# The MLA score matmuls of a page group cut in two, the first half and the values ahead of the eighth page's keys

## The chip, the cores and the metric

The kernel runs on one core of a Trainium2 chip. The metric is the device time of one execution in microseconds (us). The program is written by hand, engine by engine: each engine runs its own instruction stream, and the streams meet only at semaphores. Every engine works through its stream in order, so a wait holds back all that stands behind it on that engine.

## The reference, cut to what matters

The reference is one step of a two-layer decoder over a prompt of 1024 positions and a sample of 8 sequences with 8 new positions each. The change touches one part: the attention of the 8 sequences over their cached pages (32 pages of 128 positions each, in each layer).

```python
def page_step(carry, inp):
    phys, j = inp
    c_blk = cache_ckv[layer, phys]                  # 128 x 256
    kpe_blk = cache_kpe[layer, phys]                # 128 x 32
    k = _mla_keys(c_blk, kpe_blk, pos, w_uk, g_k)   # RMS norm over [c_blk @ w_uk, kpe], then rotation
    sc = jnp.einsum('bthd,bphd->bhtp', q, k).astype(jnp.float32) * MLA_SCALE
    return _online_update(carry, sc, c_blk), None   # running maximum, running sum, p @ c_blk
```

The kernel never forms the normed keys. It folds the query into the latent space (`qt`), takes the scores from the page itself, and multiplies them afterwards by one factor for each position and head. That factor needs the sum of squares of `c_blk @ w_uk`, so the product is still made for every page, for its squares alone.

## The kernel before, in words

Each layer has a prompt stage, then the sample stage, then the output projection. The sample stage goes through 32 groups (`k` = 0 to 31) of G = 8 pages (`j` = 0 to 7), four groups to a sequence; both layers together have 64 groups. In a group, with "page 1" for `j` = 0 and so on:

- **TensorE** (`pe_group`, L1837 to L1869) turns pages two at a time (`turn_pair`, L1784, 4 transposes), and makes the keys of each page (`keys`, L1797: 2 matmuls of 512 columns, which the profile shows as 4 records). The next pair is turned two pages ahead of its use; the next group's first pair is turned ahead of page 8's keys (L1854). The rotated positional keys are transposed at page 2 (L1860), the last group's maxima at page 4 (`maxima_T`, L1831), the maxima are spread over the partitions at page 6 (`maxima_over`, L1835). Behind page 8's keys stand all scores of the group (`scores_of`, L1813 and L1815: for each page 6 matmuls of 64 columns with 64 weight columns, 12 records of the profile) and then the values of the last group (`values`, L1826: 8 matmuls with 64 weight columns, 16 records). Weights of all keys and turns are 128 columns wide, those of scores and values are 64 wide. `sample_step` (L1668) puts other small pieces of the sample's work between the pages.
- **ScalarE** copies each turned pair out of PSUM (L785), squares the keys (L806), and in the next group takes the exponentials of the scores at page 6 (`softmax`, L817 and L818), behind page 6's squaring and ahead of page 7's. L818 ends with the semaphore `pp_ready`, on which `values` waits. At the group's end it makes a logarithm and an exponential for the root (L810, L811).
- **VectorE** reduces the squares (L1299). After page 8's it computes the factor (L1304 to L1310), waits for `ps_ps`, the end of the scores, multiplies the scores out of PSUM bank 4 (L1316) and takes the maxima (L1318, `pm_ready`). Then it adds the last group's values to the accumulator (`gather`, L1342), and begins the next group with the sum of squares of the positional keys (L1297). `softmax` at pages 4 and 6 has the running maximum (L1327 to L1332) and the subtraction (L1335).
- **SyncE** loads pages into a ring of 4 groups. A group's slot is reloaded when `ring_free` tells that its values are done.

`keys` of page j waits for the squaring of page j - 2 (two PSUM banks), and the squaring of page j waits for VectorE's reduction of page j - 2 (two SBUF buffers). `scores_of` waits for `rotT_evac`, which ScalarE gives at page 3, and in group 0 for `qt_ready`, which VectorE gives at page 7 after copying the folded query (L1211, waiting for L1696 of TensorE at page 6). In group 3 ScalarE has four pieces of gate work, the last of them (L760) behind L818, and VectorE has two (L1241, L1244).

After group 31, TensorE turns the first rows of the mixed output (`turn_rows(0)`, L1422), then `maxima_T(31)` and the output projection (L1890). The projection waits for VectorE's copy of the turned rows (L1351), which stands on VectorE behind all of group 31 and the `gather` of group 30.

The few lines that fix TensorE's order at a group's end:

```python
                        if j == G - 1 and k + 1 < DB * NG:
                            turn_pair(k + 1, 0)
                        keys(k, j)
...
                    scores_of(k)
                    if k:
                        values(k - 1)
```

Of the kernel before, what the change touches and what calls it, by code (L numbers as in the profile page):

```python
# [29 lines left out]
DB, DT = 8, 8  # L30
# [31 lines left out]
G = 8  # L62
NG = PAGES // G
# [29 lines left out]
def build(nc, a, out):  # L93
    ctx = ExitStack()
    with ctx:
# [3 lines left out]
        s = type("Semaphores", (), {n: ctx.enter_context(nc.semaphore(n)) for n in SEMAPHORES})  # L99
# [107 lines left out]
        def pcT(q):  # L207

            q %= 5
            return pairs_r[:, q, :] if q < 3 else pairs_x[:, q - 3, :]  # L210
# [34 lines left out]
        def pages_of(k):  # L245

            return cring[:, k % NG, :, :] if k < DB * NG - 2 else late[:, k - (DB * NG - 2), :, :]
# [1151 lines left out]
        def _(pe):  # L1399
            mm, tp = pe.matmul, pe.transpose  # L1400

            def halves(out, lhsT, rhs, T, start, stop):

                for c in range(0, T, 64):
                    ins = mm(out[c:c + 64], lhsT[:, c:c + 64], rhs, start=start, stop=stop)
                return ins
# [57 lines left out]
            for L in range(DEPTH):  # L1464
# [38 lines left out]
                for t in range(NT):  # L1503
# [22 lines left out]
                    for c in range(2):  # L1526
                        ins = tp(ps[:, 6, 256 + c * P:256 + c * P + T], mq[0:T, c * P:c * P + P], ident[0:T, 0:T])
                    ins.then_inc(s.mqT_ps, 1)
                    if pm_:
# [5 lines left out]
                        for h in range(MH):  # L1535
                            w = slice(MD * (h % 2), MD * (h % 2) + MD)
                            ins = mm(ps[:, 6 + h % 2, NM * (h // 2):NM * (h // 2) + NM], mqT[w, h // 2, :], mkT[w, h // 2, :], start=True, stop=True)
# [11 lines left out]
                    for c in range(2):  # L1549
                        ins = tp(ps[:, 2, c * P:c * P + T], ck[0:T, c * P:c * P + P], ident[0:T, 0:T])  # L1550
# [21 lines left out]
                    for c in range(2):  # L1572
                        ins = mm(ps[0:T, 0, :], cT[:, c, 0:T], w_uk[:, c, :], start=c == 0, stop=c == 1)
                    ins.then_inc(s.kn_ps, 1)
                    if pm_:
                        pe.wait_ge(s.mp_ready, m + 1)
                        for j in range(8):
                            ins = tp(ps[:, 6 + j // 4, (j % 4) * P:(j % 4) * P + P], pt[:, 0, j * P:j * P + P], ident[:])
                        ins.then_inc(s.mpT_ps, 1)
                    pe.wait_ge(s.cq_ready, n + 1)  # L1580
                    for c in range(3):
                        ins = tp(ps[:, 3, c * P:c * P + T], cq[0:T, c * P:c * P + P], ident[0:T, 0:T])
# [7 lines left out]
                    for e in range(2):  # L1590
                        for c in range(3):
                            ins = mm(ps[0:T, 2 + e, 0:4 * QK], cqT[:, c, 0:T], w_uq[:, c, 4 * QK * e:4 * QK * e + 4 * QK], start=c == 0, stop=c == 2)
                    ins.then_inc(s.q_ps, 1)

                    if pm_:
# [3 lines left out]
                        for h in range(MH):  # L1599
                            for c in range(2):  # L1600
                                ins = halves(ps[:, 5, 256 + MD * h:256 + MD * h + MD], ptT[:, 2 * h + c, :], mv[:, c, MD * h:MD * h + MD], P, c == 0, c == 1)
                        ins.then_inc(s.mo_ps, 1)
                        pe.wait_ge(s.k_ready, n + 1)
                        for h in range(H):
                            ins = tp(ps[0:QK, h // 4, (h % 4) * P:(h % 4) * P + P], qk[:, 1, QK * h:QK * h + QK], ident[:])
# [3 lines left out]
                        for h in range(H):  # L1609
                            ins = tp(ps[0:QK, 2 + h // 4, (h % 4) * P:(h % 4) * P + P], qk[:, 0, QK * h:QK * h + QK], ident[:])  # L1610
                        ins.then_inc(s.kqv_ps, 1)
                        pe.wait_ge(s.kT_evac, m + 1)
                        for c in range(2):
                            ins = mm(ps[:, 1, :], cT[:, c, :], w_uv[:, c, :], start=c == 0, stop=c == 1)
# [19 lines left out]
                        for h in range(H):  # L1634
                            nh = m * H + h
                            pe.wait_ge(s.p_ready, nh + 1)
                            for j in range(t + 1):
                                ins = tp(ps[:, j // 4, (j % 4) * P:(j % 4) * P + P], pt[:, h % 2, j * P:j * P + P], ident[:])  # L1638
# [19 lines left out]
                            for j in range(t + 1):  # L1658
                                ins = halves(ps[:, 2, VD * h:VD * h + VD], ptT[:, j, :], vv[:, j, VD * h:VD * h + VD], P, j == 0, j == t)
# [113 lines left out]
                def turn_pair(k, q):  # L1773

                    n = (L * DB * NG + k) * (G // 2) + q
                    g = k % NG
                    if q == 0:
                        pe.wait_ge(bulk_in[g], 32 + ((L * DB * NG + k) // NG + 1) * 2 * G * 16)
                    if n >= 2:

                        pe.wait_ge(s.pcT_evac, n - 1)
                    for j in range(2):
                        for c in range(2):
                            ins = tp(ps[:, q % 2, j * R + c * P:j * R + c * P + P], pages_of(k)[:, 2 * q + j, c * P:c * P + P], ident[:])  # L1784
                    ins.then_inc(s.pcT_ps, 1)

                def keys(k, j):

                    np_ = (L * DB * NG + k) * G + j
                    pe.wait_ge(s.pcT_evac, np_ // 2 + 1)  # L1790
                    if np_ >= 2:

                        pe.wait_ge(s.pkn_sq, np_ - 1)
                    page = pcT(k * (G // 2) + j // 2)
                    for c in range(2):
                        o_ = (j % 2) * R + c * P
                        ins = mm(ps[:, 2 + j % 2, :], page[:, o_:o_ + P], w_uk[:, c, :], start=c == 0, stop=c == 1)  # L1797
                    ins.then_inc(s.pkn_ps, 1)

                def scores_of(k):  # L1800

                    n0, b = L * DB * NG + k, k // NG
                    pe.wait_ge(s.rotT_evac, n0 + 1)
                    if k == 0:
                        pe.wait_ge(s.qt_ready, L + 1)
                    for j in range(G):
                        page = pcT(k * (G // 2) + j // 2)
                        for c in range(3):
                            for half in range(0, P, 64):
                                so = ps[half:half + 64, 4, 64 * j:64 * j + 64]  # L1810
                                if c < 2:
                                    o_ = (j % 2) * R + c * P + half
                                    ins = mm(so, page[:, o_:o_ + 64], qt[:, c, 64 * b:64 * b + 64], start=c == 0, stop=False)  # L1813
                                else:
                                    ins = mm(so, rotT[:, j // 4, half:half + 64], qrz[:, j % 4, 64 * b:64 * b + 64], start=False, stop=True)  # L1815
                    ins.then_inc(s.ps_ps, 1)

                def values(k):

                    n0, g = L * DB * NG + k, k % NG  # L1820
                    pe.wait_ge(s.pp_ready, n0 + 1)
                    if n0:
                        pe.wait_ge(s.pacc_ready, n0)
                    for i in range(G):
                        e = 64 * (i % 2)
                        ins = mm(ps[e:e + 64, 6, 0:RW], psb[:, k % 2, 64 * i:64 * i + 64], pages_of(k)[:, i, :], start=i < 2, stop=i >= G - 2)  # L1826
                    ins.then_inc(s.ring_free, 1)

                def maxima_T(k):
                    pe.wait_ge(s.pm_ready, L * DB * NG + k + 1)  # L1830
                    tp(ps[:, 7, 256:384], pm, ident[:]).then_inc(s.pmT_ps, 1)  # L1831
# [5 lines left out]
                def pe_group(k):  # L1837

                    n0 = L * DB * NG + k
                    if k == 0:  # L1840
                        pe.wait_ge(s.q_ready, NT * L + TP + 1)
                        turn_pair(0, 0)
                    for j in range(G):
                        sample_step(k, j)
                        if j % 2 == 0 and j + 2 < G:
                            if j:
                                keys(k, j)
                                turn_pair(k, j // 2 + 1)
                            else:
                                turn_pair(k, 1)  # L1850
                                keys(k, j)
                            continue
                        if j == G - 1 and k + 1 < DB * NG:
                            turn_pair(k + 1, 0)  # L1854
                        keys(k, j)
                        if j == 1:

                            pe.wait_ge(s.kpe_rot, n0 + 1)
                            for c in range(2):
                                ins = tp(ps[:, 7, c * P:c * P + P], krot[:, k % 2, c * P:c * P + P], ident[:])  # L1860
                            ins.then_inc(s.rotT_ps, 1)
                        if j == 3 and k:
                            pe.wait_ge(s.rotT_evac, n0 + 1)
                            maxima_T(k - 1)
                        if j == 5 and k:
                            maxima_over(k - 1)
                    scores_of(k)
                    if k:
                        values(k - 1)  # L1869

                for k in range(DB * NG):
                    pe_group(k)
# [42 lines left out]
                for b in range(DB):  # L1915
                    for c in range(2):
                        o_ = (2 * b + c) * 64
                        ins = mm(ps[:, 6 + o_ // 512, o_ % 512:o_ % 512 + 64], acc[:, b, c * P:c * P + P], fold[:, 0:64], start=True, stop=True)  # L1918
# [4 lines left out]
                for h in range(H):  # L1923
                    for c in range(2):
                        ins = mm(ps[0:TS, 5, VD * h:VD * h + VD], latT[:, (c * H + h) * TS:(c * H + h) * TS + TS], w_uv[:, c, VD * h:VD * h + VD], start=c == 0, stop=c == 1)
# [10 lines left out]
                for k in range(KD):  # L1936
                    for c in range(2):
                        ins = mm(ps[TS * c:TS * c + TS, 2, :], m_T[p][:, k, 0:TS], w_out[:, k, 512 * c:512 * c + 512], start=k == 0, stop=k == KD - 1)  # L1938
# [59 lines left out]
```

## Time and profile before

| what | value |
|---|---|
| median of 3 runs | 3035.79 us (3029.9 to 3035.99) |
| the profiled execution | 3033.12 us |
| its span | 3031.3 us |
| granted TensorE clock, mean over the span | 0.992 |
| PE (TensorE matmul) busy | 2949.8 us (97%) |
| PEld (weight load) busy | 1800.4 us (59%) |
| DVE (VectorE) busy | 1589.8 us (52%) |
| ACT (ScalarE) busy | 1037.7 us (34%) |
| keys, L1797 | 587.7 + 376.7 us, 2048 records, 598 ns each |
| scores, L1813 and L1815 | 146.9 + 115.1 + 74.7 us, 6144 records |
| values, L1826 (without the 64 records that read w_in) | 114.5 us, 960 records, 379 ns each |

The times of a row in a timeline are the start from the beginning of the span and the duration of the merged piece. Matmuls overlap in the pipeline, so what a piece costs is read from the start of the next piece less its own start. PEld rows are weight loads; in a run of equal matmuls they start ahead of the matmul that uses them. "[0.96 <-DVE xT L1351]" means that the engine sat idle for 0.96 us before the row and that the named line of VectorE ended the wait.

### The profile page before, as it was taken

Reading aid. Unit: us, or ns where it says so; the run is one execution under the profiler, and the core shown is the slowest. Engines: PE = TensorE matmul, PEld = TensorE weight load, DVE = VectorE, ACT = ScalarE, POOL = GpSimd, SP = SyncE. Lnnn points to the kernel's source line nnn. Section 1 sums busy time; section 2 is a strip of 40 time slices with the busy share of each in tenths; the row PEclk is TensorE's granted clock in tenths of the full one; section 3 lists DMA queues with packets and bytes.
Section 4 is the critical chain, followed back from the end, with each engine's and each line's share of the span. In section 5 each row is a group of like instructions: output and inputs, shape, how many; then the busy total and the mean of one; then the engine's idle time right before and its main releaser. Section 6 shows DMA issues by size and latency. Waiting matters only on the chain. (4 is left out here: it accounts for less than half of the span.)

```text
span 3031.3 us, 55947 instructions
## 1 busy us (share of the span) xinstructions
PE 2949.8 (97%) x20261; PEld 1800.4 (59%) x20261; DVE 1589.8 (52%) x3547; ACT 1037.7 (34%) x2159; POOL 328.1 (11%) x465
## 2 busy tenths in 40 slices
PE   7999999999999999999999999999899999999999
PEld 4666666755555555555456667666455555555554
DVE  3665655545665555554145656565456555555531
ACT  1333333323434444442023333333234344444410
POOL 1110000001111111110000000000111111111100
PEclk9999999999999999999999999999999999999999
DMA  6000000013212222222520000000421222222322
GB/s 267 31 17 17 17 17 17 14 52 105 52 48 60 55 58 56 61 79 112 193 93 17 17 17 17 17 17 13 121 53 50 54 61 56 57 56 58 102 85 80
DMA packets 192166, 179.57 MB, mean 59 GB/s; under 512 B 93769, under 2 KB 171666, under 8 KB 189842
## 3 DMA queue, kind: packets, MB, share of 16 engines
q1 hardware_dynamic: 190144, 175.18, 18.8%
q8 instruction: 162, 2.65, 0.4%
q14 instruction: 114, 0.93, 0.1%
q10 hardware_dynamic: 1746, 0.81, 0.1%
HBM read 153.41 MB, written 22.50 MB: 58 GB/s over the span
## 5 line engine op out<-in xcount | busy, mean ns | idle before, releaser
L1299 DVE TENSOR_REDUCE w_in<-w_in 128x8 f32<-128x512 f32 x512 | 351.4, 686 | 551.0 <-ACT w_in L806 547.5
L1797 PE MATMUL ps<-w_uk,region 128*128 128x512 f32 x1248 | 587.7, 598 | 1.1
L1411 PE MATMUL ps<-w_in,xT 128*128 128x256 f32 (+9 forms) x1952 | 546.9, 434 | 2.9 <-DVE xT L925 2.9
L1411 PEld LDWEIGHTS ps<-w_in,xT 128*128 128x128 f32 (+1 forms) x1952 | 352.9, 185 | 157.0 <-issue 74.3
L806 ACT ACTIVATE w_in<-ps 128x512 f32<-128x512 f32 x512 | 305.7, 597 | 211.0 <-PE ps L1797 195.0
L1797 PE MATMUL ps<-w_uk,xT 128*128 128x512 f32 x800 | 376.7, 598 | 0.8 <-ACT w_in L806 0.3
L1797 PEld LDWEIGHTS ps<-w_uk,region 128*128 128x128 f32 x1248 | 216.6, 191 | 191.9 <-issue 191.0
L537 POOL TENSOR_TENSOR rs<-us,mhalf 128x1 f32<-128x1 f32 (+4 forms) x132 | 130.9, 991 | 1414.3 <-DVE us L965 757.8
L1797 PEld LDWEIGHTS ps<-w_uk,xT 128*128 128x128 f32 x800 | 139.3, 192 | 125.0 <-issue 125.0
L1784 PEld LDWEIGHTS ps<-ident,region 128*128 128x128 f32 x960 | 116.2, 141 | 108.5 <-issue 108.1
L785 ACT COPY region<-ps 128x512 f32<-128x512 f32 x156 | 91.3, 585 | 259.9 <-PE ps L1784 258.6
L1151 DVE COPY U<-ps 128x512 f32<-128x512 f32 (+3 forms) x128 | 75.7, 592 | 150.3 <-PE ps L1638 148.5
L1784 PE MATMUL ps<-ident,region 128*128 128x128 f32 x960 | 147.0, 276 | 0.0
L1815 PE MATMUL ps<-U,region 128*64 128x64 f32 x2048 | 146.9, 222 | 0.0
L1624 PE MATMUL ps<-region,W 96*128 96x512 f32 (+3 forms) x384 | 145.9, 493 | 0.0
L1140 DVE TENSOR_REDUCE st<-ps 128x1 f32<-128x256 f32 (+7 forms) x128 | 97.0, 758 | 81.8 <-PE ps L1625 78.0
L583 POOL TENSOR_TENSOR xt<-region,mkv 128x128 f32<-128x128 f32 x64 | 29.2, 456 | 1021.4 <-issue 787.6
L715 ACT ACTIVATE U<-ps,us 128x256 f32<-128x256 f32 (+7 forms) x128 | 94.8, 740 | 124.4 <-DVE us L1141 86.2
L1813 PEld LDWEIGHTS ps<-U,region 128*64 128x64 f32 x2496 | 99.5, 138 | 28.8 <-issue 28.8
L1890 PE MATMUL ps<-region,xT 128*128 128x512 f32 x256 | 114.4, 595 | 1.9 <-DVE xT L1351 1.9
L1813 PE MATMUL ps<-U,region 128*64 128x64 f32 x2496 | 115.1, 223 | 0.0
L1826 PE MATMUL ps<-region 128*64 128x257 f32 x960 | 114.5, 379 | 0.0
(390 smaller groups left out, 3889.9 us busy)
## 6 DMA issues: line engine op xcount, KB each, us to landing
region<-in_cache_ckv SPq DMA_DIRECT2D x480, 128.0 KB, 2.0
w_in<-in_w_in SPq DMA_DIRECT2D x16, 1240.0 KB, 11.6
mix_rows<-xn SPq DMA_DIRECT2D x16, 512.0 KB, 2.9
region<-in_cache_kpe SPq DMA_DIRECT2D x512, 16.0 KB, 1.7
region<-in_w_out SPq DMA_DIRECT2D x8, 1024.0 KB
xt<-in_x_prompt SPq DMA_DIRECT2D x11, 512.0 KB, 4.0
xt<-x_mid SPq DMA_DIRECT2D x11, 512.0 KB, 4.2
region<-in_w_mem_kv SPq DMA_DIRECT2D x2, 2048.0 KB, 24.2
```

What stands on the lines that cost most here:

```text
L537: pool.tensor_tensor(rs[0:T, c:c + k], us[0:T, c:c + k], mhalf[0:T, 0:k], ALU.pow).then_inc(s.root_ready, 1)
L806: tell(act.activation(sqb[:, j % 2, :], ps[:, 2 + j % 2, :], ACT.Square), s.pkn_sq, np_)
L1140: own(dve.tensor_reduce(st[:, 62 + h % 2:63 + h % 2], src, X, ALU.max))
L1299: tell(dve.tensor_reduce(pst[:, 0, j * H:j * H + H], heads(sqb[:, j % 2, :], H), X, ALU.add), s.pkn_red, np_)
L1411: ins = mm(out, xT[:, k, 0:T], w_in[:, k, c0:c0 + w], start=k == 0, stop=k == KD - 1)
L1624: ins = mm(ps[:, bank + c // 512, 0:w], qT[:, h, :], kT[:, h, c:c + w], start=True, stop=not last)
L1784: ins = tp(ps[:, q % 2, j * R + c * P:j * R + c * P + P], pages_of(k)[:, 2 * q + j, c * P:c * P + P], ident[:])
L1797: ins = mm(ps[:, 2 + j % 2, :], page[:, o_:o_ + P], w_uk[:, c, :], start=c == 0, stop=c == 1)
L1813: ins = mm(so, page[:, o_:o_ + 64], qt[:, c, 64 * b:64 * b + 64], start=c == 0, stop=False)
L1815: ins = mm(so, rotT[:, j // 4, half:half + 64], qrz[:, j % 4, 64 * b:64 * b + 64], start=False, stop=True)
L1826: ins = mm(ps[e:e + 64, 6, 0:RW], psb[:, k % 2, 64 * i:64 * i + 64], pages_of(k)[:, i, :], start=i < 2, stop=i >= G - 2)
L1890: ins = mm(ps[:, 2 + c, :], m_T[p][:, k, :], w_out[:, k, 512 * c:512 * c + 512], start=k == 0, stop=k == KD - 1)
```

## The change

TensorE's order at the end of a group is rewritten. `scores_of` takes a first and a last page. Ahead of page 8's keys, and ahead of the turn of the next group's first pair, stand now the scores of pages 1 to 4 and the values of the last group. The scores of pages 5 to 8 stand at the end of the group, alone, and only they signal `ps_ps`. No other engine's stream is touched, and no instruction is added or taken away except that the second call of `scores_of` repeats the waits at its head.

```diff
-                def scores_of(k):
+                def scores_of(k, j0, j1):
...
-                    for j in range(G):
+                    for j in range(j0, j1):
...
-                    ins.then_inc(s.ps_ps, 1)
+                    if j1 == G:
+                        ins.then_inc(s.ps_ps, 1)
...
-                        if j == G - 1 and k + 1 < DB * NG:
-                            turn_pair(k + 1, 0)
+                        if j == G - 1:
+                            scores_of(k, 0, G // 2)
+                            if k:
+                                values(k - 1)
+                            if k + 1 < DB * NG:
+                                turn_pair(k + 1, 0)
                         keys(k, j)
...
-                    scores_of(k)
-                    if k:
-                        values(k - 1)
+                    scores_of(k, G // 2, G)
```

## Rows read from the trace of the kernel before

**Rows 1.** Windows view: us; busy PE, PEld, DVE, ACT, POOL; clock; DMA share, GB/s.

```profile
716.00:1400.00 684.00, 681.69 (x5396) 386.06 (x5397) 373.57 (x813) 285.18 (x547) 91.33 (x152) 1.00 0.22 60
```

**Rows 2.** Waits view, TensorE: total us, times, longest.

```profile
PE ps L1890 <- DVE xT L1351: 1.9, 2, 1.0
```

**Rows 3.** Timeline, TensorE, end of group 21, layer 1: start, duration, line, shapes.

```profile
1182.71 1.88 PE L1797 MATMUL ps<-w_uk,region 128*128 128x512 f32 x4
1184.43 0.60 PE L1784 MATMUL ps<-ident,region 128*128 128x128 f32 x4
1184.86 1.88 PE L1797 MATMUL ps<-w_uk,region 128*128 128x512 f32 x4
1186.68 0.45 PE L1813 MATMUL ps<-U,xT 128*64 128x64 f32 x8
...
1187.08 0.40 PE L1813 MATMUL ps<-U,xT 128*64 128x64 f32 x8
...
1189.53 1.91 PE L1826 MATMUL ps<-region 128*64 128x257 f32 x16
1191.36 0.66 PE L1784 MATMUL ps<-ident,region 128*128 128x128 f32 x4
1191.86 3.60 PE L1797 MATMUL ps<-w_uk,xT 128*128 128x512 f32 x8
```

**Rows 4.** Timeline, weight loads in the same stretch.

```profile
1184.76 0.30 PEld L1797 LDWEIGHTS ps<-w_uk,region 128*128 128x128 f32 x2
...
1186.67 0.31 PEld L1813 LDWEIGHTS ps<-U,xT 128*64 128x64 f32 x8 [0.76 <-issue]
```

**Rows 5.** Chain of waits, group 3 of layer 2: start, piece's time, line.

```profile
2281.13 1.74 PE ps L1826 x16
2282.87 3.45 PE ps L1721 x16
```

**Rows 6.** Timeline, TensorE, start of group 1, layer 2.

```profile
2211.90 0.38 PE L1703 MATMUL ps<-cT,U 128*64 128x8 f32 x4
2212.13 0.26 PE L1703 MATMUL ps<-rk,U 128*64 128x8 f32 x2
2212.32 0.66 PE L1784 MATMUL ps<-ident,region 128*128 128x128 f32 x4
```

**Rows 7.** Timeline, ScalarE and VectorE, group 21 and start of group 22.

```profile
1185.17 0.63 ACT L818 ACTIVATE region<-region 128x512 f32<-128x512 f32 x1
...
1190.70 0.69 DVE L1316 TENSOR_TENSOR region<-ps,w_in 128x512 f32<-128x512 f32 x1
...
1198.94 1.29 ACT L806 ACTIVATE w_in<-ps 128x512 f32<-128x512 f32 x2
```

**Rows 8.** Timeline, group 0 of layers 1 and 2: query copies and TensorE after page 7's keys.

```profile
713.87 1.80 DVE L1211 COPY U<-ps 128x256 f32<-128x256 f32 x4
713.92 0.60 PE L1784 MATMUL ps<-ident,region 128*128 128x128 f32 x4
...
2203.77 1.80 DVE L1211 COPY U<-ps 128x256 f32<-128x256 f32 x4
...
2204.38 0.60 PE L1784 MATMUL ps<-ident,region 128*128 128x128 f32 x4
```

**Rows 9.** Timeline, group 3 of layer 1.

```profile
787.08 0.60 PE L1784 MATMUL ps<-ident,region 128*128 128x128 f32 x4
...
788.90 0.63 ACT L818 ACTIVATE region<-region 128x512 f32<-128x512 f32 x1
```

**Rows 10.** Timeline, group 31 of layer 2 and the start of the projection.

```profile
2886.18 0.45 PE L1813 MATMUL ps<-U,xT 128*64 128x64 f32 x8
...
2890.12 0.69 DVE L1316 TENSOR_TENSOR region<-ps,w_in 128x512 f32<-128x512 f32 x1
...
2892.46 0.69 DVE L1351 COPY xT<-ps 128x512 f32<-128x512 f32 x1
...
2893.25 3.67 PE L1890 MATMUL ps<-region,xT 128*128 128x512 f32 x8 [0.96 <-DVE xT L1351]
```

## The prediction

> **What bounds the kernel now.** I read the page first: TensorE is busy for 97% of the span, VectorE for half, ScalarE for a third. Then the windows view of the sample stage, the only stage that the change touches: in 684 us TensorE is busy for 681.69, at the full granted clock, and the DMA engines are used to 22% [rows 1]. The waits view then says what is left to win: no line of the group loop has a TensorE wait in its list worth more than a few microseconds in all, and the one at the stage's end, the projection waiting for VectorE's copy, has 1.9 us over both layers [rows 2]. So the bound is the order and the price of TensorE's own instructions, and a reordering can win only where two neighbours cost something at their border. Last I read the timeline of one ordinary group's end [rows 3], piece by piece, from start to start. The reader should see that all borders are free except two:
>
> - Page 7's keys to the turn: 1184.43 - 1182.71 = 1.72 us for 4 records, 0.43 each; the long run behind the next turn shows the same spacing (8 records, 3.60 to the end of the last). Turn to keys: 0.43. No border cost.
> - Page 8's keys to the scores: 1186.68 - 1184.86 = 1.82, so 0.10 more; and the first page of scores takes 0.40, where the seven behind it take (1189.53 - 1187.08) / 7 = 0.35, so 0.05 more. **Entering** the block of 64-wide weights costs 0.15.
> - Values to the next turn: 1191.36 - 1189.53 = 1.83. Where values are followed by another piece with 64-wide weights they take 1.74 [rows 5], so 0.09 more; and the turn takes 0.50 in place of 0.43, so 0.07 more. **Leaving** costs 0.16.
>
> Scores to values has no border cost that I can see.
>
> **The change, part by part.** The order keys 7, turn, keys 8, scores, values, next turn becomes keys 7, half scores, values, turn, keys 8, half scores, next turn. The count of matmuls is the same. The border keys 7 to turn (free) goes; another entering and another leaving come.
>
> 1. *Borders.* Entering is 0.15, as above. Leaving straight from scores is not in the trace; the nearest rows are L1703, pieces of the same kind: the last two records take 2212.32 - 2212.13 = 0.19, where four take 2212.13 - 2211.90 = 0.23, so two 0.12; that is 0.07, and with the slower turn 0.14 [rows 6]; leaving from values is 0.16. These are the two bounds; I take 0.15. Group 0 (no values) and group 31 (no turn) have the same borders. 64 groups x 0.30 = 19.2 us, all on TensorE and so all on the path. The lower bound of this term is 0 (the split borders hide), the upper 64 x 0.31 = 20.
> 2. *The wait of the values for the exponentials.* Today they start at 1189.53, and L818 is done at 1185.17 + 0.63 = 1185.80 [rows 3, 7], so 3.7 us of cover. Now they are due at 1184.43 + 0.10 + 0.05 + 4 x 0.35 = 1185.98. Cover left: 0.18 us, in group 21 and likewise in the ordinary groups, since they all repeat it. From the end of L1351, 2892.46 + 0.69 = 2893.15, to the matmul that waited for it TensorE takes 0.10 us [rows 10], so I cost this at 0, on a knife's edge. Lower bound 0; upper bound see the second rival. Nothing in this stretch helps TensorE: all that stands behind the values, the turn and page 8's keys, would be late with them.
> 3. *Group 3*, where the exponentials are late behind gate work: L818 ends at 788.90 + 0.63 = 789.53, values due at 787.08 + 1.55 = 788.63 [rows 9]. Stall 0.9, with some 0.05 for the signal 0.95; two layers: 1.9 us.
> 4. *Group 0*, where the scores wait for the folded query. VectorE's four copies end at 713.87 + 1.80 = 715.67 and at 2203.77 + 1.80 = 2205.57; the first scores are due 0.10 behind page 7's keys, at 714.02 and 2204.48 [rows 8]. Today page 8's keys lie between and cover it. Stalls 1.7 and 1.15: 2.9 us, with nothing behind it to absorb it, since TensorE has no idle time.
> 5. *VectorE's chain behind page 8.* Page 8's keys now end 1.45 + 1.83 + 0.16 = 3.4 us later, and the multiplication L1316 follows them by 3.9 to 4.0 us as today (4.02 in group 21 [rows 3, 7], 3.94 in group 31 [rows 10]), since it hangs on squaring, reduction and root and not on the scores. So it now starts some 2.5 us behind the end of the scores, and the whole of VectorE's group end slides 3.2 us into the next group. Who is late? The first is the squaring of page 3, which needs page 1's reduction: due at 1198.94 [rows 7]. VectorE: L1316 at 1190.04 + 3.9 = 1193.9, then 0.7, 1.05, gather 0.5, L1297 0.45, page 1's reduction 0.7: 1197.4. Slack 1.5 us. The transposed maxima come later still. Cost 0, for all groups but perhaps group 3 (VectorE is full there), where I keep 0 to 1 us. The pages' loads on SyncE start earlier, since `ring_free` does; the queues have room [rows 1]; 0.
> 6. *The stage's end.* In group 31 the slide has nothing to hide in. Page 8's keys ended at 2886.18 and the projection began at 2893.25, waiting for VectorE [rows 10]: 7.1 us behind. That chain keeps its length, and page 8's keys now end 3.4 us later, of which 0.3 is already in term 1 and 0.1 is won because page 8's squaring is no longer queued behind the exponentials. TensorE waits 3.0 us more, in each layer: 6.0 us. Bounds 5 and 7.
>
> Sum: 19.2 + 0 + 1.9 + 2.9 + 0 + 6.0 = **30 us slower**. Against the profiled execution's 3033.1 that is 3063; the median of the runs stands 2.7 above it, so 3065.8, and I say **3065**.
>
> TensorE's weight loads [rows 4] show why the border costs: ahead of keys the load starts 0.10 before the matmul, ahead of the first scores both start together, after 0.76 in which no weights were loaded. Here the Trainium skill has two rules that point in opposite ways. "TensorEngine Tiling (Array Packing)", Key Properties, says that a change of the tiling mode drains the engine; by it the price belongs to the change of weight width and comes again at each new border, which gives the sum above. "TensorE: Matmul & The Clock Gate", The mechanism, says that the engine pulls a weight load ahead of running matmuls where it goes to a free part of the array or the background buffer; by it the new borders would hide, which is the first rival. The rows bear out the first of the two at the old borders.
>
> **The rivals.**
> - *The new borders are free* (the price is paid once a group whatever the order, say by the first use of a bank). Then only terms 3, 4 and 6 are left: +10.8, 3046. For it: nothing but that the exact border scores to turn is not in the trace. Against: 0.15 and 0.16 are seen at three different kinds of neighbours [rows 3, 6].
> - *The knife's edge falls the wrong way.* If the exponentials' signal reaches TensorE later than 0.18 us behind L818, each group stalls, and page 8's keys move with it, but the exponentials themselves hang on page 6 and do not, so it does not grow. 0.1 to 0.25 us x 62 groups = 6 to 15 us: 3072 to 3080. For it: there is no reserve in any group, and a small delay of VectorE's subtraction ahead of it would do. Against: the release that rows 10 show took 0.10.
> - *Faster.* The border price belongs not to the width but to the waits at a block's head: weights aren't fetched past a wait that came true only lately. In the new order the waits of the half scores and of the turns are long true, and then the old borders' 0.31 go too: 64 x 0.31 = -20, and with +10.8 it is -9: 3027. It decides where the first scores' weight load starts. Against it: keys and turns have waits at their heads too, and their loads run ahead [rows 4]; `rotT_evac` was true pages earlier. Little for it.
> - The change can't fail to do what it says, since TensorE's order is written out.
>
> **How the numbers follow.** Forecast (3055 to 3071) 0.65; borders free 0.10; knife's edge 0.16; faster 0.04; 0.05 for something between that ends within 0.2%, about what a measurement of this kernel can tell from no change (6 us). Faster 0.04, same 0.05, slower 0.91. The range takes in the free borders at its low end, 3046, and most of the knife's edge, 3078.
>
> **What the profile of the changed kernel would show.** Term 1: 1.82 from keys 7 and from keys 8 to the scores behind them, a turn of 0.50 behind both the values and the second half, and an ordinary group 0.30 us longer than before, from its first score to the next group's. Term 2: values starting 1.55 behind the end of keys 7, with no wait for L818 in the list; about 1 us there in group 3. Term 4: a wait of the first scores for L1211, 2.9 in all. Term 5: L1316 3.9 behind the keys' end, no TensorE wait at pages 3 to 5 that is new. Term 6: the projection's wait for L1351 near 1.9 + 6, part of it perhaps shown at L1831. I am wrong if an ordinary group is no longer than before, or if the values wait in every group.

## The result and the profile after

The changed kernel takes 3073.11 us (median of 4 runs, 3069.47 to 3079.41) against 3032.85 us for the kernel before in the same comparison: ratio 1.0136, 95% interval 1.0111 to 1.0162, so 40 us slower. In a later comparison it gave 1.0125 (1.0109 to 1.0142). The forecast was 3065, slower, with a range of 3046 to 3078.

| what | before | after |
|---|---|---|
| the profiled execution | 3033.12 us | 3079.41 us |
| its span | 3031.3 us | 3077.6 us |
| mean granted TensorE clock | 0.992 | 0.987 |
| PE busy | 2949.8 us | 2982.4 us |
| PE matmul records | 20261 | 20261 |

The profiled execution is the longest of the four. First, an ordinary group's end in TensorE's timeline, group 21 of layer 1 (start, duration, line; the rows of L1815, which lie between those of L1813, are left out). It answers to [rows 3]. From the values on, line numbers are a little higher than in the kernel before: L1827 was L1826, L1832 was L1831, L1893 was L1890.

```profile
1198.24 1.88 PE L1797 MATMUL ps<-w_uk,region 128*128 128x512 f32 x4
1200.05 0.45 PE L1813 MATMUL ps<-U,xT 128*64 128x64 f32 x8
...
1200.45 0.40 PE L1813 MATMUL ps<-U,xT 128*64 128x64 f32 x8
...
1201.50 1.91 PE L1827 MATMUL ps<-region 128*64 128x257 f32 x16
1203.34 0.66 PE L1784 MATMUL ps<-ident,region 128*128 128x128 f32 x4
1203.83 1.88 PE L1797 MATMUL ps<-w_uk,region 128*128 128x512 f32 x4
1205.64 0.45 PE L1813 MATMUL ps<-U,region 128*64 128x64 f32 x8
...
1206.74 0.40 PE L1813 MATMUL ps<-U,region 128*64 128x64 f32 x8
...
1207.19 0.66 PE L1784 MATMUL ps<-ident,region 128*128 128x128 f32 x4
1207.68 3.60 PE L1797 MATMUL ps<-w_uk,xT 128*128 128x512 f32 x8
```

Both kinds of border are there twice. Into the scores: 1200.05 - 1198.24 = 1.81 behind page 7's keys and 1205.64 - 1203.83 = 1.81 behind page 8's, where 1.72 is the plain price, and a first page of 0.40 each time. Out of them: from the last page of the second half to the turn 1207.19 - 1206.74 = 0.45 where a page takes 0.35, and the turn 0.49. The border scores to turn, which the trace of before did not have, costs 0.10 + 0.06 = 0.16. From one group's transposes at page 2 to the next group's, the timeline has 21.14 us before and 21.44 after, in each of groups 19 to 30.

TensorE's weight loads in the same stretch, the first of each half:

```profile
1200.05 0.31 PEld L1813 LDWEIGHTS ps<-U,xT 128*64 128x64 f32 x8 [0.76 <-issue]
...
1205.64 0.31 PEld L1813 LDWEIGHTS ps<-U,region 128*64 128x64 f32 x8 [0.76 <-issue]
```

Both start together with their matmuls, after 0.76 without a load, as at the one border of before [rows 4]. The rival on the faster side had the first of them running ahead, since what it waits for was given pages earlier; it does not.

The second view is ScalarE's and VectorE's timeline of the same group, the rows that answer to [rows 7].

```profile
1200.70 0.63 ACT L818 ACTIVATE region<-region 128x512 f32<-128x512 f32 x1
```

```profile
1209.42 0.69 DVE L1316 TENSOR_TENSOR region<-ps,w_in 128x512 f32<-128x512 f32 x1
```

L818 is done at 1201.33 and the values start at 1201.50, with no wait: 0.17 of cover, as forecast. L1316 starts 1209.42 - 1205.64 = 3.8 behind the end of page 8's keys, 2.3 behind the end of the scores.

The third is TensorE's list of waits (total us, times, longest), the lines that are new or longer than before; it answers to [rows 2].

```profile
PE ps L1832 <- DVE w_in L1318: 5.9, 2, 2.9
PE ps L1714 <- DVE ws L1230: 4.9, 4, 2.1
...
PE ps L1813 <- DVE U L1211: 2.3, 2, 1.2
...
PE ps L1893 <- issue: 1.8, 2, 1.0
PE ps L1827 <- ACT region L818: 1.6, 2, 0.8
```

L1832 is `maxima_T` at the stage's end, L1813 the first scores of group 0, L1827 the values in group 3: three waits that were forecast. L1893, the projection, waits as before (1.9 there [rows 2]). L1714 was not forecast: before, the same line had 0.8 us in all. Where it waits, in layer 2's group 2, TensorE:

```profile
2264.66 0.65 PE L1714 MATMUL ps<-ck,w_in 64*64 64x257 f32 x2
...
2269.67 0.64 PE L1714 MATMUL ps<-ck,w_in 64*64 64x257 f32 x2 [2.05 <-DVE ws L1230]
```

and VectorE in the same stretch:

```profile
2267.61 1.02 DVE L1318 TENSOR_REDUCE w_in<-region 128x128 f32<-128x512 f32 x1
2268.68 0.48 DVE L1342 SCALAR_TENSOR_TENSOR ws<-ws,w_in,ps 128x257 f32<-128x257 f32 x1
2269.19 0.42 DVE L1230 COPY ws<-ps 64x257 f32<-64x257 f32 x1
```

The piece at page 2 writes the PSUM bank that L1230 has yet to empty from page 1's piece, and L1230 stands on VectorE behind the end of group 1, which now comes later.

Last, the windows view of layer 1 around the same place (length, busy time of PE, PEld, DVE, ACT, POOL, granted clock, DMA share, GB/s):

```profile
751.00:754.20 3.20, 1.15 (x4) 0.32 (x3) 3.00 (x6) 0.60 (x1) 0.00 (x0) 0.98 0.39 93
754.20:764.00 9.80, 9.80 (x15) 3.60 (x16) 2.47 (x5) 0.60 (x1) 2.98 (x5) 0.50 0.17 45
```

Behind the wait, in which TensorE was busy for 1.15 of 3.20 us, it gets 0.50 of its clock, 1.2 GHz in place of 2.4, for 9.8 us. Behind the same wait in layer 2 it does not:

```profile
2266.54:2269.74 3.20, 1.15 (x4) 0.27 (x3) 2.99 (x7) 0.63 (x2) 0.00 (x0) 1.00 0.31 88
2269.74:2279.54 9.80, 9.39 (x29) 3.99 (x30) 4.18 (x8) 2.75 (x5) 2.98 (x5) 1.00 0.22 59
```

So groups 1 and 2 together are 7.48 us longer than before in layer 1 and 2.57 in layer 2, with the same wait of 2.05 in both. The whole difference then adds up. The mean clock of 0.987 means 2 x 0.013 x 3078 = 80 us at 1.2 GHz, that of 0.992 some 50 us. I take half of the difference, some 14 to 15 us, as time lost; that is an estimate, and experiment nine shows that it can be too much. Borders 64 x 0.30 = 19.2; waits 5.9 + (4.9 - 0.8) + 2.3 + 1.6 = 13.9; clock 14. That is 47, and the spans differ by 46.3.

### The profile page after: what moved, and what is told of

Same layout as the page of the kernel before. It is cut to its first block and busy times, and to the rows that moved or that the text cites. A ratio compares the mean times of both kernels' runs of the same rounds, so it can differ in the third digit from the quotient of the medians.

```text
span 3077.6 us, 55949 instructions
## 1 busy us (share of the span) xinstructions
PE 2982.4 (97%) x20261; PEld 1806.5 (59%) x20261; DVE 1590.9 (52%) x3547; ACT 1038.8 (34%) x2159; POOL 328.7 (11%) x465
## 5 line engine op out<-in xcount | busy, mean ns | idle before, releaser
L806 ACT ACTIVATE w_in<-ps 128x512 f32<-128x512 f32 x512 | 305.9, 597 | 285.7 <-PE ps L1797 269.2
L1815 PE MATMUL ps<-U,region 128*64 128x64 f32 x2048 | 147.2, 222 | 0.0
L1813 PEld LDWEIGHTS ps<-U,region 128*64 128x64 f32 x2496 | 99.5, 138 | 61.5 <-issue 61.5
L1813 PE MATMUL ps<-U,region 128*64 128x64 f32 x2496 | 118.6, 225 | 2.3 <-DVE U L1211 2.3
L1893 PE MATMUL ps<-region,xT 128*128 128x512 f32 x256 | 118.4, 612 | 1.8 <-issue 1.8
L1827 PE MATMUL ps<-region 128*64 128x257 f32 x960 | 114.6, 380 | 1.6 <-ACT region L818 1.6
```

Source lines behind the costliest of these rows:

```text
L806: tell(act.activation(sqb[:, j % 2, :], ps[:, 2 + j % 2, :], ACT.Square), s.pkn_sq, np_)
L1893: ins = mm(ps[:, 2 + c, :], m_T[p][:, k, :], w_out[:, k, 512 * c:512 * c + 512], start=k == 0, stop=k == KD - 1)
```

## The experiments

**One.** The change in groups 4 to 30 alone.

```diff
                         if j == G - 1:
-                            scores_of(k, 0, G // 2)
-                            if k:
-                                values(k - 1)
+                            if 4 <= k < DB * NG - 1:
+                                scores_of(k, 0, G // 2)
+                                if k:
+                                    values(k - 1)
...
-                    scores_of(k, G // 2, G)
+                    if 4 <= k < DB * NG - 1:
+                        scores_of(k, G // 2, G)
+                    else:
+                        scores_of(k, 0, G)
+                        if k:
+                            values(k - 1)
```

> The change is made in groups 4 to 30 of each layer alone (54 groups); groups 0 to 3 and 31 keep the order of before. Theory (each new border of weight width costs 0.15, and one-time waits sit at the ends): each of these groups 0.30 us longer, 16.2 us in all, no new TensorE wait and no new low-clock stretch near a new wait; ratio to before about 1.0053. Rival (borders free, the whole loss is waits and clock): ratio 1.000. Rival (the knife's edge costs something in every group): over 0.35 a group and L818 in TensorE's wait list.

Measured: 3045.08 us, ratio 1.0055 (1.0042 to 1.0069). Each of the 54 groups is 0.30 us longer (one of them 0.51), the other groups are as before, but for group 0 of both layers, 1.6 shorter, where the clock fell less. TensorE's list of waits has nothing new; the lines of this stage in it:

```profile
PE ps L1899 <- DVE xT L1351: 1.9, 2, 1.0
PE ps L1714 <- DVE w_in L1226: 1.8, 2, 0.9
...
PE ps L1714 <- DVE ws L1230: 0.8, 2, 0.4
```

So some 16 us (54 x 0.30) come with no wait at all, by the borders. The mean clock, 0.994, is not below before's; the profiled execution is only 10.9 us longer, because less of it ran at 1.2 GHz (37 us against 50).

**Two.** The complement, with the condition `not 4 <= k < DB * NG - 1`: groups 0 to 3 and 31.

> The complement: the change in groups 0 to 3 and 31 of each layer alone (10 groups). Theory: 3 us of borders, and all the waits: group 0 some 1.2 each, page 2 of group 2 some 2 each, group 3 some 1 each, the stage's end 2.9 each, together 14 us, so 17 us, plus what stretches of low clock behind these waits cost (0 to 12 us); ratio 1.006 to 1.009. If the two halves don't add up to the whole change's 1.0136 within the intervals, something couples them. Rival (borders are all): 1.001.

Measured: 3055.69 us, ratio 1.0084 (1.0071 to 1.0098), 25 us. The list of waits is the whole change's: L1832 5.9, L1714 4.9, L1827 1.6, and L1813 3.5 us. The two halves add up: 0.0055 + 0.0084 = 0.0139 against 0.0136. Its profiled span, 3050.6 at a mean clock of 0.992, is 19.3 over before's: 3 of borders and 15 of waits, with about as much time at 1.2 GHz as before (51 us against 50). Its other runs have spans 3 to 5 us longer, at a mean clock of 0.990 to 0.991. By the medians ten groups cost more than the other 54. Behind the wait of 2.05 us the clock stays at 1.00 in layer 1 here, and falls for 3.4 us in layer 2: the other way round than in the change.

**Three.** The cut without the move: both calls at the place of before.

```diff
-                    scores_of(k)
+                    scores_of(k, 0, G // 2)
+                    scores_of(k, G // 2, G)
                     if k:
                         values(k - 1)
```

> The scores are cut into two calls that stand at the place of before, one behind the other, with the values behind them; only the second call's repeated wait is new. Theory (the border price hangs on the change of weight width): same as before, groups unchanged within 0.01 us, ratio 1.000. Rival (a block's head with its waits costs something by itself): up to 0.15 a group, 10 us, ratio 1.003.

Measured: 3032.83 us, ratio 1.0007 (0.9998 to 1.0017), and each group as long as before to 0.01 us. The repeated wait at a block's head costs nothing by itself; this takes the ground from the rival of this experiment. The prediction's own rival, by which only a wait that came true lately costs, is not tried here, but the change answers it: the semaphore of the first half is given pages earlier, and the entry costs 0.10 all the same.

**Four.** The scores cut as in the change, the values at the end.

```diff
                         if j == G - 1:
                             scores_of(k, 0, G // 2)
-                            if k:
-                                values(k - 1)
...
                     scores_of(k, G // 2, G)
+                    if k:
+                        values(k - 1)
```

> The scores are cut as in the change, but the values stay at the group's end behind the second half. As many borders as in the change. Theory: ordinary groups 0.30 us longer (19.2 in all); no wait for L818 in group 3; group 0 as in the change (1.2 each); page 8's keys end only 1.55 later than before, not 3.4, so the wait at page 2 of group 2 falls to about 0.2 and that at the stage's end by 1.8 each; total about 19.2 + 2.4 + 0.4 + 2.2 = 24 us, ratio 1.008. Rival (values ahead of the keys are what costs, through PSUM or the ring's earlier loads): ordinary groups under 0.15 longer.

Measured: 3052.51 us, ratio 1.0073 (1.0058 to 1.0089). Ordinary groups are again 0.30 longer. No wait for L818 is left; L1832 falls from 5.9 to 2.4 and L1714 for L1230 from 4.9 to 1.5; L1813 has 3.5. So where the values stand decides how far VectorE slides, and not the border price.

**Five.** In groups 4 to 30 three parts, the first two pages ahead of page 7's keys. The edit is shown against experiment one's kernel, and so is the next one.

```diff
                         if j == G - 1:
                             if 4 <= k < DB * NG - 1:
-                                scores_of(k, 0, G // 2)
+                                scores_of(k, G // 4, G // 2)
                                 values(k - 1)
...
+                        if j == G - 2 and 4 <= k < DB * NG - 1:
+                            scores_of(k, 0, G // 4)
                         keys(k, j)
```

> In groups 4 to 30 (54 groups) the scores are cut in three: pages 1 and 2 ahead of page 7's keys, pages 3 and 4 with the values ahead of page 8's, the rest at the end; the other groups as before. One more border pair than the change has. Theory (0.30 for each pair): these groups 0.60 us longer than before, 32.4 us in all, ratio 1.0107; ScalarE gets the exponentials done no later, and the values are due 0.15 later than in the change, so no wait for L818. Rival (only the first cut costs, or a short block hides its entry): 0.30 to 0.45 a group.

Measured: 3064.8 us, ratio 1.0111 (1.0096 to 1.0126); the groups are 0.64 longer, not 0.60. No new wait. The dose is doubled and so is the price. TensorE's timeline shows the extra pair of borders:

```profile
1192.61 0.38 PE L1836 MATMUL ps<-w_in,ones 128*128 128x128 f32 x2
1192.92 0.45 PE L1813 MATMUL ps<-U,xT 128*64 128x64 f32 x8
...
1193.32 0.40 PE L1813 MATMUL ps<-U,xT 128*64 128x64 f32 x8
...
1193.77 1.98 PE L1797 MATMUL ps<-w_uk,region 128*128 128x512 f32 x4
1195.68 0.45 PE L1813 MATMUL ps<-U,region 128*64 128x64 f32 x8
```

The extra pair is 0.34: entry 0.09 (0.31 from the small matmul's start, which keys follow at 0.22), 0.05 on the first page (0.40), exit 1193.77 - 1193.32 - 0.35 = 0.10, and the keys behind it take 1.91, of which 0.10 is the entry to the next block, as ever, and 0.09 their own slow start. Keys as the first piece behind an exit lose 0.09 where a turn loses 0.06.

**Six.** In groups 4 to 30 two pages in the first part, six in the second.

```diff
-                                scores_of(k, 0, G // 2)
+                                scores_of(k, 0, G // 4)
...
-                        scores_of(k, G // 2, G)
+                        scores_of(k, G // 4, G)
```

> In groups 4 to 30 only pages 1 and 2 are scored ahead of the values, six at the end; the other groups as before. The borders are those of the change, but the values are due 0.70 us sooner behind page 7's keys. Theory (the change has 0.18 us of cover left for the exponentials, of which the signal to TensorE takes 0.05 to 0.1): the values wait for L818 in every such group, 0.57 to 0.62 us beyond 0.30, so the groups are 0.87 to 0.92 longer, 47 to 50 us in all, ratio 1.016. Rival (the cover was larger than I read, or ScalarE catches up): under 0.5 longer.

Measured: 3082.48 us, ratio 1.0167 (1.0152 to 1.0183); the groups are 0.93 longer. TensorE's list of waits begins with

```profile
PE ps L1827 <- ACT region L818: 22.6, 54, 0.7
```

one for every such group, and a group's timeline, TensorE and then ScalarE, shows how close it is:

```profile
1202.33 0.45 PE L1813 MATMUL ps<-U,xT 128*64 128x64 f32 x8
...
1202.73 0.40 PE L1813 MATMUL ps<-U,xT 128*64 128x64 f32 x8
...
1203.66 1.96 PE L1827 MATMUL ps<-region 128*64 128x257 f32 x16 [0.41 <-ACT region L818]
```

```profile
1202.98 0.63 ACT L818 ACTIVATE region<-region 128x512 f32<-128x512 f32 x1
```

L818 ends at 1203.61 and the values start 0.05 later. They are due at 1202.73 + 0.35 = 1203.08, so 0.58 late, and take 0.05 more. In the change they are due 0.70 later: the reserve there is 0.70 - 0.58 = 0.12 us, and the knife's edge holds in every ordinary group.

**Seven.** The kernel before with one step of ScalarE moved. The ground for it is the kernel before's own timeline at pages 3 to 5 of group 22, TensorE and then ScalarE:

```profile
1199.38 0.27 PE L1831 MATMUL ps<-ident,w_in 128*128 128x128 f32 x1
...
1199.68 1.96 PE L1797 MATMUL ps<-w_uk,region 128*128 128x512 f32 x4
...
1201.47 0.60 PE L1784 MATMUL ps<-ident,region 128*128 128x128 f32 x4
```

```profile
1198.54 0.37 ACT L799 COPY region<-ps 128x256 f32<-128x256 f32 x1
```

The squaring of page 3 starts behind L799 at 1198.94 [rows 7] and releases page 5's keys at about 1199.6.

```diff
-                        if j == 2:
-                            act.wait_ge(s.rotT_ps, n0 + 1)
-                            tell(act.copy(rotT, ...), s.rotT_evac, n0)
...
                         tell(act.activation(sqb[:, j % 2, :], ps[:, 2 + j % 2, :], ACT.Square), s.pkn_sq, np_)
+                        if j == 1:
+                            act.wait_ge(s.rotT_ps, n0 + 1)
+                            tell(act.copy(rotT, ...), s.rotT_evac, n0)
```

> The kernel before, with one step of ScalarE moved: the copy of the transposed positional keys (L799) from page 3, behind the copy of the third pair, to the end of page 2, behind page 2's squaring, where ScalarE is idle. In the kernel before, page 5's keys start 0.30 us behind the maxima's transpose where other neighbours need 0.11, because the squaring of page 3 ends late behind L799. Theory (that gap is a wait on ScalarE, 0.19 us): each group 0.19 us shorter, about 12 us in all, ratio 0.996. Rival (the 0.11 is the turn of one record by itself, no wait): unchanged, 1.000.

Measured: 3016.18 us, ratio 0.9953 (0.9939 to 0.9966): the only version that beats both kernels. Ordinary groups are 0.26 shorter, more than expected. Its timeline, TensorE and then ScalarE (the copy is now L806, the squaring L803):

```profile
1190.27 0.27 PE L1831 MATMUL ps<-ident,w_in 128*128 128x128 f32 x1
...
1190.38 1.88 PE L1797 MATMUL ps<-w_uk,region 128*128 128x512 f32 x4
...
```

```profile
1187.05 0.37 ACT L806 COPY region<-ps 128x256 f32<-128x256 f32 x1
...
1189.42 0.60 ACT L803 ACTIVATE w_in<-ps 128x512 f32<-128x512 f32 x1
```

The gap behind L1831 goes from 0.30 to 0.11, and the keys themselves from 1201.47 - 1199.68 = 1.79 to 1.72 (the next turn starts at 1192.10): that is the other 0.07. The waits view of before never named this wait, since its 0.19 us are hidden in the modelled end of the matmul in front of it.

**Eight.** The same step in the changed kernel.

> The changed kernel with the same step of ScalarE moved. Theory: the gain of 0.19 us a group is independent of the cut, so an ordinary group is 0.11 us longer than before's and the whole is 12 us faster than the changed kernel, ratio to before about 1.009. Rival (the exponentials, due at page 7, lose their 0.18 us of cover because TensorE reaches page 7 sooner behind page 6): the exponentials hang on page 6's spreading of the maxima, which moves with TensorE, so I expect no new wait; if one appears it shows as L818 in TensorE's list and eats the gain.

Measured: 3056.65 us, ratio 1.0084 (1.0068 to 1.0099). Ordinary groups are 0.04 longer than before, 0.30 - 0.26; L818 has 1.5 us in the list, both times in group 3, so the exponentials kept their cover. In the ordinary groups the two effects add.

**Nine.** The changed kernel with `NEW_VALUES` in group 2 two pages later.

```diff
-NEW_VALUES = [(1, 6), (1, 7), (2, 0), (2, 1), (2, 2), (2, 3), (2, 4), (3, 0)]
+NEW_VALUES = [(1, 6), (1, 7), (2, 2), (2, 3), (2, 4), (2, 5), (2, 6), (3, 0)]
```

> The changed kernel with the five small pieces of new values in group 2 each moved from pages 1 to 5 to pages 3 to 7 (the last to page 7). Theory (the new wait of 2.05 us at page 2 of group 2 is VectorE's copy L1230 at page 1, which stands behind VectorE's late end of group 1): at page 3 VectorE has caught up, the wait goes, 4.1 us less in all, and with it any stretch of low clock that it brings; group 1 to 2 only 0.30 longer than in the kernel before, ratio to the changed kernel about 0.998. Rival (VectorE is behind for longer): the wait moves along with the pieces.

Measured: 3066.05 us, ratio 1.0112 (1.0095 to 1.0129). L1714's wait for L1230 is back to before's 0.8 us, and groups 1 and 2 together are 0.63 longer than before, which is two border pairs. The profile has a clock of 0.991 and a span of 3065.4, 12.2 under the change's; 4.1 of it is the wait, and most of the rest is low clock that fell away in groups 0 and 2 of layer 1. In all it has 24 us less at 1.2 GHz, so half of that, 12, is more than the 8 us that are left for it: some of that time must stand where the low clock costs less than half. Layer 1's groups 1 and 2 gain 6.85 us, layer 2's 1.94, which is the wait alone. Against the change's 3071.55 to 3073.11 the median is 5 to 7 us lower, but the intervals of the two ratios overlap; what shows the gain is the timeline.

**Ten.** The change once more.

> The changed kernel once more, unaltered. Theory: the work and waits are the same to 0.01 us in an ordinary group, and profiled executions differ by half of their difference in low-clock time: this one has fewer than the 79.6 us of the first profile, so it ends at 3077.6 less half of that difference. Over 5 rounds the ratio to before is 1.012 to 1.014. Rival (something other than the clock made the first profile long): a difference beyond that, seen in ordinary groups.

Measured: 3071.55 us (3065.43 to 3079.32), ratio 1.0125 (1.0109 to 1.0142). I had expected less time at the low clock in this profile; it had the same mean, 0.987, and the same span, 3077.5. Its other runs ended at spans of 3069.0, 3063.6 and 3070.5 with 0.992, 0.993 and 0.990. So one program spreads by 14 us with nothing but the clock differing in the records (of the runs without a profile these have only span and clock), and the longest runs are those of the lowest clock.

## Why the prediction was right, point by point

- *Term 1, borders, 19.2 us.* Right to 0.01 a group. The split borders did not hide (first rival): a third part cost another 0.34. They did not hang on waits (the rival on the faster side): the pure cut cost nothing, and the first half pays its entry though its semaphore is long given. That the price belongs to the width of the weights, 64 against 128, fits every border seen, with keys, turns, a small matmul and values as neighbours; but no run changed the width alone, so this is argued and not shown.
- *Term 2, the exponentials, 0.* Right: no wait in ordinary groups. The reserve is 0.12 us, measured by taking away 0.70.
- *Term 3, group 3, 1.9.* Measured 1.6 in the list, and the group 1.03 longer beyond its border, twice.
- *Term 4, group 0, 2.9.* Measured 2.3 in the change, where TensorE itself came later to page 7, and 3.5 in experiments two and four. In the change the clock was low for 6.8 us just ahead of it in both layers, and the waits are 1.1 and 1.2; in experiments two and four it was not, and they are 1.7. The trace of before had such a stretch in layer 2, so the forecast took one of each; that its 2.9 lies between is luck.
- *Term 5, VectorE's slide.* This is the step that failed. I followed it to the squaring of page 3 and wrote "Cost 0, for all groups but perhaps group 3". The slide was right (L1316 moved 2.9 us into the next group, against 3.2), and that squaring was not late: it starts 3.65 us behind page 2's transposes in both traces. But in group 2 the small step L1230 stands on VectorE behind the same late end, and L1714 waits for it: 2.05 us in each layer. I had listed who waits for VectorE's ordinary steps and not for those that `sample_step` puts between them. The sign named for this term, no new wait at pages 3 to 5, came true and missed the wait, which is at page 2.
- *Term 6, the stage's end, 6.0.* Measured 5.9, at L1832 as I had thought possible, while the projection's wait stayed as it was.
- *What no term held.* The clock. The change's profile has 29 us more at 1.2 GHz than before's, some 14 us lost. Of the stretches, 20 us stand right behind new waits: 10.2 behind L1714's in layer 1, 3.4 and 6.8 at the ends of the two stages; the rest lies elsewhere, most of it in group 0. By the medians, 40 us less 33 of borders and waits, the usual run lost about 7.

The forecast of +30 lacked 4 us of waits and the clock. The result, 3073.11, lies outside the 3055 to 3071 that had a chance of 0.65, and inside what the knife's edge would have given, 3072 to 3080. The range held it because its upper end had been set for the knife's edge, which is not what filled it: that much is luck.

## What to carry to other kernels

Where one engine is busy throughout, look at its neighbours pair by pair: the block of matmuls with narrower weights pays here at its entry and exit, and cutting it in two bought that price again; such a cut has to win a wait worth more. When an engine off the path slides by some microseconds, list every step that stands behind the slide on that engine, the rare ones of single rounds too, and ask who waits for each. A wait may be missing from the list of waits: compare the spacing of equal instructions, as the 0.30 against 0.11 behind L1831, which was worth 15 us.

## What the runs showed of the hardware that I had not expected

The price of a change between 128 and 64 weight columns hardly depends on the neighbours tried here: 0.09 to 0.10 at the entry with 0.05 on the first page, 0.09 to 0.10 at the exit, with 0.06 more on a turn that follows and 0.09 on keys.

A wait of 2 to 3 us of an otherwise full TensorE can cost more than its length, and the same wait need not. Behind the wait of 2.05 us in the change's layer 1 the granted clock was 0.50 for 9.8 us, which is some 5 us of work lost; in layer 2 it stayed at 1.00, and so it did in layer 1 of experiment two, while experiment eight has 3.4 us of low clock behind each of the two. The wait of 2.9 us at the stage's end was followed by 3.4 to 6.8 us at 0.50 in both layers of all five profiles that have it (the change twice, experiments two, eight and nine); where it is 1.2 us, in experiment four, no such stretch follows. That longer waits bring the low clock on is what these profiles suggest; what decides it behind the shorter one was not found, and the runs of one program without a profile differ in their clock too.
